# A causal mask applied after the exponential on the vector engine, with three more accumulator banks in the first feed-forward group

## What is computed

```
h = h + 0.5 * g1 * swiglu(modulate(rmsnorm(h)))     # feed-forward 1, inner width 2816
h = h + g2 * mixer(modulate(rmsnorm(h)))            # 4 differential + 4 latent attention heads
h = h + 0.5 * g3 * swiglu(modulate(rmsnorm(h)))     # feed-forward 2
out = rmsnorm(h)
# attention, per 128-query block q0 : q0+128, keys 0 : q0+128
s = q @ k.T * scale;  s = where(query >= key, s, -inf);  p = softmax(s);  o = combine(p) @ v
```

## Time and profile before

| | us |
|---|---|
| median of three runs | 3063.17 (3061.47 to 3076.46) |
| the profiled execution, its own time | 3066.18 |
| span of its slowest core (core 1) | 3064.6 |
| PE busy / DVE busy / ACT busy on that core | 2842.9 / 1403.2 / 1254.9 |

### The profile page before, as it was taken

The page is one execution under the profiler, slowest core; times in us unless marked ns, Lnnn a source line. Parts: engine busy times, 40 slices in busy tenths (PEclk is TensorE's granted clock), DMA queues, the critical chain, the costliest instruction groups (busy, mean ns, idle before and its releaser), DMA issues.

```text
span 3064.6 us, 42690 instructions; the slowest of 8 cores (3034.3 to 3064.6 us)
## 1 busy us (share of the span) xinstructions
PE 2842.9 (93%) x16528; PEld 1356.0 (44%) x16528; DVE 1403.2 (46%) x2808; ACT 1254.9 (41%) x1750; POOL 75.0 (2%) x147
## 2 busy tenths in 40 slices
PE   3799998999899999999978999999999999999998
PEld 1344443444454444544434445444454444444443
DVE  3564215344455455244446545654535443532532
ACT  2421205345434456444245443555755524322311
POOL 1000000000000000000000000000000000000000
PEclk9899999999999999999989999999999999999999
DMA  9886685475914934553883333434345278336436
GB/s 193 170 160 154 168 218 158 134 206 129 219 62 115 201 99 105 119 153 112 247 265 117 96 110 113 140 100 131 86 137 162 99 251 262 138 106 203 165 119 224
DMA packets 144138, 470.76 MB, mean 154 GB/s; under 512 B 17376, under 2 KB 21216, under 8 KB 129760
## 3 DMA queue, kind: packets, MB, share of 16 engines
q1 hardware_dynamic: 127600, 399.80, 40.9%
q0 software_dynamic: 16336, 68.23, 14.2%
HBM read 452.83 MB, written 100.66 MB: 181 GB/s over the span
## 4 chain that ended last, share of the span: by engine, by line
PE 76%; DMA 11%; ACT 5%; DVE 5%; issue 1%; SPq 1%; POOL 0%; ACTq 0%; DVEq 0%; POOLq 0%
PE psall L127 76%; ACT pt L127 3%; DMA wf<-sdn 2%; DMA wm<-w_ada 1%; DMA h<-hst 1%; DMA h<-qk 1%; DMA wf<-w_ada 1%; DMA accsb<-pos 1%; DMA hst<-xL 1%; SPq L127 1%; ACT mu L127 1%; DVE mu L127 1%; DVE ftm L127 1%; DVE accsb L127 1%; ACT L127 1%
## 5 line engine op out<-in xcount | busy, mean ns | idle before, releaser
L127 PE MATMUL psall<-uf,wf 128*128 128x512 bf16 x4224 | 1037.1, 384 | 30.5 <-DVE hst L127 6.6
L127 ACT ACTIVATE pt<-psall 128x1024 bf16<-128x1024 f32 (+3 forms) x520 | 453.0, 872 | 457.3 <-PE psall L127 455.8
L127 PEld LDWEIGHTS psall<-uf,wf 128*128 128x128 bf16 x4224 | 400.2, 99 | 462.5 <-issue 28.7
L127 PE MATMUL psall<-actf,wf 128*128 128x512 bf16 x2112 | 516.3, 386 | 16.8 <-DMA wf<-sdn 16.8
L127 ACT ACTIVATE ftf<-psall 128x512 f32<-128x512 f32 x352 | 210.1, 597 | 660.0 <-PE psall L127 645.9
L127 DVE SCALAR_TENSOR_TENSOR ftf<-ftf,psall 128x512 f32<-128x512 f32 x352 | 241.1, 685 | 448.0 <-ACT ftf L127 416.8
L127 PE MATMUL psall<-mu,wm 128*128 128x512 bf16 (+2 forms) x1312 | 328.6, 381 | 12.5 <-ACT mu L127 8.2
L127 PE MATMUL psall<-mixb,wf 128*128 128x512 bf16 x1408 | 321.4, 383 | 8.6 <-ACT mixb L127 4.9
L127 PEld LDWEIGHTS psall<-actf,wf 128*128 128x128 bf16 x2112 | 200.7, 99 | 227.6 <-issue 20.2
L127 DVE SCALAR_TENSOR_TENSOR hst<-psall,SC,hst 128x512 f32<-128x512 f32 x120 | 90.0, 750 | 426.1 <-PE psall L127 315.3
L127 DVE TENSOR_TENSOR actf<-ftf,psall 128x512 bf16<-128x512 f32 x264 | 180.9, 685 | 195.2 <-PE psall L127 192.7
(11 more groups left out here) (113 smaller groups left out, 1991.5 us busy)
## 6 DMA issues: line engine op xcount, KB each, us to landing
wf<-sgu SPq DMA_DIRECT2D x242, 512.0 KB, 3.9
wf<-sdn SPq DMA_DIRECT2D x192, 352.0 KB, 4.1
h<-hst SPq DMA_DIRECT2D x120, 256.0 KB, 4.5
xt<-h SPq DMA_DIRECT2D x30, 1024.0 KB, 7.1
wm<-w_ada POOLq DMA_DIRECT2D x32, 512.0 KB, 12.1
hst<-xL SPq DMA_DIRECT2D x64, 256.0 KB, 6.4
qk<-h SPq DMA_DIRECT2D x16, 1024.0 KB, 6.5
h<-qk SPq DMA_DIRECT2D x16, 1024.0 KB, 9.7
```

The costliest lines, as they stand in the source:

```text
L127: ins = getattr(eng, o.fn[0])(**o.fn[1])
```

## The change

The two mask matmuls of a diagonal step are left out. A new function `mask(i)` multiplies the first 128 columns of both halves of `pt` by a matrix of zeros and ones on DVE, after a minimum with 3.0e38. The constant tile holds the 0/1 matrix twice, so it grows from four to five blocks. `mask(i+1)` is emitted inside lane M's credit: after 70% of it in the ordinary branch, at its end in the branch with the transpose. The credit of an ordinary step with r > 0 goes from 0.6 to 0.8 of `W_ATT`. The pool `psF` begins with banks 5, 6, 7, 2, 3, 4 and `psM` with 0, 1; `lane_m` takes 2, 3, 4 back before the first mixer.

```diff
-        psF = Banks([5, 6, 7])
-        psM = Banks([0, 1, 2, 3, 4])
+        psF = Banks([5, 6, 7, 2, 3, 4])
+        psM = Banks([0, 1])
...
-                      start=True, stop=(not diag), skip_group_check=True)
-                if diag:
-                    for m in range(2):
-                        I("pe", "matmul", r=[cmR], w=[PR[m]], out=PS[m][:, 0:128], lhsT=ident, rhs=maskT, start=False, stop=True, skip_group_check=True)
+                      start=True, stop=True, skip_group_check=True)
...
+            def mask(i):
+
+                g, qc, j, r, last = steps[i]
+                if j >= 4 * qc:
+                    pt, ptR = state[i]
+                    v = pt[:].rearrange("p (m n) -> p m n", m=2)[:, :, 0:128]
+                    I("dve", "scalar_tensor_tensor", r=ptR + [cmR], w=ptR, out=v, in0=v, scalar=3.0e38, in1=mask2, op0=ALU.min, op1=ALU.mult)
...
             qk(0)
-            yield W_ATT
+            yield 0.7 * W_ATT
+            mask(0)
+            yield 0.3 * W_ATT
...
                     if i + 1 < n:
                         qk(i + 1)
-                    yield 0.6 * W_ATT
+                        yield 0.6 * W_ATT
+                        mask(i + 1)
...
-                    yield W_ATT * (1.0 if r == 0 else 0.6)
+                    w = W_ATT * (1.0 if r == 0 else 0.8)
+                    yield 0.7 * w
+                    if i + 1 < n:
+                        mask(i + 1)
+                    yield 0.3 * w
...
                 while s == 0 and ("grp", 0, 0, 0) not in flags:
                     yield None
+                while s == 0 and len(psM.free) < 5:
+                    for b in (2, 3, 4):
+                        if b in psF.free:
+                            psF.free.remove(b)
+                            psM.give(b)
+                    if len(psM.free) < 5:
+                        yield None
...
-    maskT = np.where(np.arange(128)[None, :] >= np.arange(128)[:, None], 0.0, -30000.0).astype(np.float32)
-    cmats = np.stack([ident, rdiff, rmla, maskT], axis=1)
+    maskT = np.where(np.arange(128)[None, :] >= np.arange(128)[:, None], 1.0, 0.0).astype(np.float32)
+    cmats = np.stack([ident, rdiff, rmla, maskT, maskT], axis=1)
```

More of the change, by code:

```diff
@@ L239, in build @@
     gsmall = din("gsmall", [128, 10])
-    cmats = din("cmats", [128, 4, 128])
+    cmats = din("cmats", [128, 5, 128])
     invf = din("invf", [128, 2])
@@ L300, in build @@
         PR = [Res(f"ps{i}", excl=True) for i in range(8)]
-        cm_sb, cmR = tile("cm_sb", [128, 4, 128], BF16)
+        cm_sb, cmR = tile("cm_sb", [128, 5, 128], BF16)
         ones_sb, onesR = tile("ones_sb", [128, 128], BF16)
@@ L318, in build @@
         rmla = cm_sb[:, 2, :]
-        maskT = cm_sb[:, 3, :]
+        mask2 = cm_sb[:, 3:5, :]
         def fpieces(t, res):
```

## The result

The changed kernel is slower: the ratio of its executions to those of the kernel before is 1.0091, 95% interval 1.0073 to 1.0110, which is 28 us (22 to 34) on 3069. Eight executions of each have medians of 3099.2 and 3069.3 us; the profiled one took 3096.8 of its own time. Medians of all executions hold some in which a die ran disturbed, so what follows goes by ratios from undisturbed ones.

What follows compares the result with a forecast made beforehand. The prediction took PE to bound the kernel (busy 2842.9 of 3064.6 us). Its terms, -23 + 32 + 23 + 2 - 2 = +32 on 3066.2, gave 3098, or 3095 by the median of the runs; range 3058 to 3126.

Steps and rivals of the forecast that it cites:

- The matmuls that go, -23: Attention's 192 diagonal steps each lose a mask matmul pair costing PE 0.12 us by distance of starts: -23 us.
- The multiply, 0.42 us: Diagonal steps gain 192 DVE multiplies of 128 x 256 bf16, 0.42 us each; about 0.29 if two columns a cycle.
- The waits, +32: Value matmuls of diagonal steps wait for exp, then DVE, holding in-order PE: +32 us, bounds 5 and 70.
- The sign that the prediction named: In attention, a new wait of value matmuls on DVE pt, some 30 us in total, would show the forecast right.
- 7 had been taken off: Diagonal steps: stalls give the next exp time and PE sometimes waits for exp anyway, so 39 us became 32.
- single deficits: Diagonal steps with one lane F chunk lack cover: 0.2 us in 29 steps, below 0.1 in others, about 8 us.
- a bad order of 0.9 us: Mask queued on DVE behind a lane F operation awaiting its chunk's last matmul: 17 steps x 0.9 = 15 us.
- The credit, +25 (+23 and +2): More lane F work in attention leaves PE idle or paced by norms: +23 after the last mixer, +2 in first sequence.
- the 3 us at the end: After the pause behind the last mixer matmul, a lower clock costs about 3 us, within the +23.
- The banks, -2: Group (0,0,0): with six banks PE may run further ahead, -2 us, bounds -6 and +3.
- the one with DVE's order as the bound: Rival in attention: masks hold DVE until exp, lane F's multiplies and banks come late; +75, 3138; chance 15%.
- Hiding the mask fully: Rival in attention: idle DVE, short exps and added credit hide the mask; -15, 3048 and below; chance 10%.

Runs made afterwards that it cites:

- e11: Kernel before with neither mask matmuls nor multiply (causal mask left out), credit 0.6, banks as before; 0.9962 of the kernel before.
- e1: Changed kernel without the multiply on DVE, causal mask left out, everything else the same; 0.9977 of the kernel before.
- e3: Kernel before with only the mask as a multiply on DVE, credit 0.6 and banks as before; 1.0061 of the kernel before.
- e6: Changed kernel with each mask emitted right after the score and value matmuls, ahead of queued coefficient operations and lane F's chunk; 1.0041 of the kernel before.
- e2: Kernel before with only the credit of later diagonal steps raised from 0.6 to 0.8; 1.0040 of the kernel before.
- e4: Kernel before with only the three banks lent to the first feed-forward group; 0.9992 of the kernel before.
- e9: Kernel before with the mask on DVE as tensor_tensor and emitted first, coefficient operations spread, credit 0.6, banks as before; 0.9981 of the kernel before.

## Why the prediction was right, and where it was not

The forecast was 3095 and slower; measured 3099.2, or by ratio 1.0091 against 1.0104. The mechanism was right: PE waits for the multiply, more than the matmuls had cost, and the moved work costs something of its own. That the total came out so near is partly luck, as not every term behind it was right.

- *The matmuls that go, -23.* Measured -12 (-27 to +4) directly, and -17 (-28 to -6) by adding up. The 0.12 us between starts is right for one step, and 23 is inside both ranges, so a shortfall is not shown. If there is one, no wait for exp is seen to take it: core 1 waits 55.0 us for ACT pt with no mask at all, and 55.6 before. The busy sum of 54.7 was the wrong price. The Trainium skill (Perfetto Trace Analysis, Identifying the Most-Contended Engine) calls matmul busy time no good measure of how close a kernel is to roofline, as pipelined matmuls look smaller in a trace. It doesn't speak of the price of a removed matmul, and here the busy sum is the larger figure, so it is e11 that decides between the two, not the page.
- *The multiply, 0.42 us.* Measured 0.422. By the Trainium skill (VectorE: DVE Perf Modes, What auto-detection actually checks) an operation whose tensors are all 16 bit may take two columns a cycle, if the firmware enables this for it, as it does for tensor_tensor. For tensor_tensor the run agrees (288 ns). The 422 ns of scalar_tensor_tensor lie on the line of 1.04 ns a column that the forecast drew through the forms of the kernel before, so no such mode shows.
- *The waits, +32.* Measured 35 (27 to 43; e1 against the changed kernel) and 30 (13 to 47; e3 against e11). The size was right, its make-up not. The sign that the prediction named, some 30 us of value matmuls waiting for DVE pt, came out as 49 on core 1 and 58 on core 7. The wait took over 11 us of others, and 7 had been taken off for that. I counted single deficits and a bad order of 0.9 us, and 5 us stalls behind ten coefficient operations or behind a DVE operation that waits for a DMA were in no term. The first kind makes 18 of 49 us on core 1. e6 shows that the order was the larger part.
- *The credit, +25 (+23 and +2).* This step failed in size: e2 measured 12 (8 to 17). I let 28.8 of lead arrive at the end. Only half did (72 matmuls, 15.6 us), since lane M in the second mixer waits for the flag of the last tile that group (0,1,13) writes, and the lead of the first sequence ends there. At the end PE pauses 3.2 us and is paced for 5, instead of 20 in all. The lead of the first sequence was not free where it ended: PE then waits 15 to 24 us at a time for down weights, by core, instead of 8 to 12, which I had put at +2. Why the weights land later there, with the DMA engines busy 97% of that stretch, no run takes apart. That the moved work shortens the waits for exp by some 14 us (e2) was in no term either, nor was the clock, but for the 3 us at the end.
- *The banks, -2.* e4 says -2.5 (-10 to +6).

Together by the runs: -17 + 35 + 12 - 2 = +28. This sum closes by construction, as the -17 is worked out from the other runs; the check that could have failed is that of e3, e2 and e4 above (0.0093 against 0.0091). Against these sizes the forecast took 6 us too much off for the matmuls, 3 too little for the waits and 13 too much for the credit, and the first two partly cancel the third.

The range's low end, 3058, is not the sum that it is said to be: the low bounds give -23 + 5 + 5 + 2 - 2 = -13, so 3050 from the median and 3053 from the profiled execution's time. The measured time is inside either way.

Of the rivals the one with DVE's order as the bound was not so wrong in kind: the wait for DVE pt on core 7 is 68.8 us, 58.2 of it for masks. It did not come through lane F's banks, though: PE's wait for DVE ftf is 2.2 us. Hiding the mask fully did not happen at any setting; e9 comes close, with 7 us of waits for masks left on core 1.

## What to carry to other kernels

A small operation moved off the bound engine is paid by whatever stands before it in its new engine's queue: read that queue at the moment when its input is ready, also for operations that wait for DMAs, and emit the new one first, and look at what then comes late behind it. When a planner's weight is changed with an edit, time the weight alone; moving work under one phase takes cover from another. Price a removed matmul by the distance of starts (23 us here), not by its busy sum (54.7, which the runs exclude). And before a tuned version is credited to the edit, run its other improvements without the edit; here that run is missing.

## What was not expected of the hardware

The same multiply of 128 x 256 bf16 by a bf16 matrix takes 422 ns as scalar_tensor_tensor with a constant and 288 ns as tensor_tensor, mean of 192 each. And a hand-over between engines is short here: 0.03 us from the end of an ACT operation to a DVE that waits for it, 0.06 us from the end of a DVE operation to a waiting PE.
